# Down projections in products of 384 columns: three with the high weights in place of four of 288

## The chip, the cores and the metric

The kernel runs on one core of one Trainium2 chip. The metric is the device time of one execution in microseconds, the median of several; lower is better.

## The reference, cut to what matters

One inference step of a two-layer decoder trunk on 512 prompt tokens and 64 sample tokens (8 sequences of 8), so 576 columns of activations, with a model width of 1024. It has four feed-forward blocks of this form, which are the part that is changed:

```python
def swiglu(h, w_gu, w_d):              # D_FF = 2816
    gu = h @ w_gu
    g, u = gu[..., :D_FF], gu[..., D_FF:]
    return (jax.nn.silu(g) * u) @ w_d

x = x + 0.5 * mod[:, 2, None] * swiglu(hh, ffn_w_gu[l, 0], ffn_w_d[l, 0])
```

Besides them there are a recurrent mixer (RG-LRU), one shared K/V projection, a differential-attention mixer with a paged cache, and norms with a shift, scale and gate per sequence. Everything is float32.

## The kernel before, in words

Activations lie transposed: 128 features on the partitions, 576 tokens along the row, `KT` = 8 such tiles for the width of 1024. For accuracy each float32 factor is split into a high and a low float32r part, and a product is made as high x high + high x low + low x high: weights `w_hi`, `w_lo`, activations `hh_hi`, `hh_lo` (after a norm) or `h_hi`, `h_lo` (inside a block).

A list, `plan`, holds the stages in order. An FFN is cut into three chunks of its inner width (8, 8 and 6 tiles). For each chunk an `up` stage makes the tiles of `h`, and a `down` stage multiplies them with the chunk's rows of the down weights and adds the result, times the gate, to the residual `x`. The last chunk's down stage (`sums=True`) also collects the sums for the next norm. The projections `w_out` and `w_o` of the two mixers are `down` stages with sums as well.

A stage consists of units. One unit is one weight block of 8 (or 6) k tiles by 256 columns, in two buffers by parity `j`: SyncE loads `raw[j]`, ScalarE rounds it to `w_hi[j]` (L808), VectorE subtracts to `w_lo[j]` (L1226), TensorE multiplies. A down stage has four units; each has two halves `t` (128 output features each). For each half and each k `tile_products` (L471 to L486) issues six float32r matmuls of 288 columns: for n = 0, 1 the high weights with the high and with the low part (L481), then the low weights with the high part for n = 0, 1 (L484). The results of half `t` accumulate in PSUM banks `2t` and `2t+1` (288 columns each). The weight is loaded anew for every matmul. "Group" below means the six products of one k and one half.

VectorE's `residual` takes a finished half: columns 0 to 287 (L1331), 288 to 511 (L1333), and the 64 sample columns in two steps through `r_tmp`, because their gate differs by sequence (L1337, L1341). The last of them frees the banks (`s0_free` for half 0, `s1_free` for half 1); TensorE waits for `s0_free` before half 0 of the next unit and for `s1_free` before its half 1. VectorE's order in a down unit is: split of the next unit's weights, residual of half 0, residual of half 1.

In the first unit of a down stage TensorE waits per k for `h_lo`, which GpSimd makes (L1654) from what VectorE (`hf`, L1385) and ScalarE (`h_hi`, L918) produced at the end of the up stage. Banks 4 and 5 are used by the conditioning projections ("bursts", L458 and L467) that are strewn over certain units; banks 6 and 7 by the norm statistics and by attention.

Of the kernel before, what the change touches and what calls it, by code (L numbers as in the profile page):

```python
# [30 lines left out]
P = 128  # L31
D_MODEL = 1024
SEQ = 512
# [19 lines left out]
PB = SEQ - TH  # L53
NC_ = 1 + DEC_BATCH
N_PAGES = PAST_LEN // PAGE
PADS = CONV_W - 1
# [50 lines left out]
def trunk(nc, consts, xT, page_table, ada_w, w_gu, w_d8, w_d6, w_in, w_gate, w_out, w_kv, w_q, w_o, k_cache, v_cache,  # L107
          yT, conv_out, h_out, kT_out, v_prompt, v_sample):
    plan = []
    count = {"u": 0, "norm": 0, "stat": 1, "h": 0, "res": 0, "rope": 0}  # L110

# [9 lines left out]
    def down(**more):  # L121

        stage("down", 4, row=0, **more)
        count["res"] += 8
        if more["sums"]:
            count["stat"] += 1

    def ffn(layer, which):
# [36 lines left out]
    with ExitStack() as ctx:  # L165
# [53 lines left out]
        def laid(key, below, *tensors):  # L219
            with ExitStack() as part:  # L220
# [10 lines left out]
        laid("linear", 0, ("hh_hi", [P, KT, T], F32R), ("hh_lo", [P, KT, T], F32R),  # L231
             ("h_hi", [P, KT, T], F32R), ("h_lo", [P, KT, T], F32R),
             ("ada", [P, GROUP, KT, 256], F32))
# [18 lines left out]
        R = region  # L252
        hh_hi, hh_lo, h_hi, h_lo = R["hh_hi"], R["hh_lo"], R["h_hi"], R["h_lo"]
        ada, ada_pro = R["ada"], R["ada_pro"]
# [51 lines left out]
        for name in ("cst_in", "x_in", "pt_in", "cond_ready", "setup_done", "setup_exp", "setup_step", "raw_full0",  # L306
                     "raw_full1", "w_hi", "out0_full", "ada_full", "pro_full", "ada_done", "ada_rows", "ada_evac",
                     "cst_late", "gate_ready", "c_zero", "os_rows", "rg_gelu", "ada_turned", "sq_full", "sq_sum",
                     "sq_last", "half_full", "res_half", "sums_full", "rstd_ready", "ln_ready", "mod_ready", "norm_t",
                     "norm_hi", "norm_lo", "norm_sv", "norm_sx", "norm_shi", "norm_s", "hh_free", "y_ready", "out_y",  # L310
                     "h_hi", "gw_full0", "gw_full1", "rope_swap", "rope_t2",
                     "kh_full0", "kh_full1", "vh_full0", "vh_full1", "sc_full", "masked",
                     "coef_ready", "att_part", "s_small", "k_full0", "k_full1", *[f"v_full{i}" for i in range(N_PAGES)],
                     "qbd_zero", "qbd_ready", "smasked", "smax", "snmx", "srs", "so_sq", "so_ln", "so_sum",
                     "so_rs", "so_n", "ss_sq", "ss_sum", "ss_ln", "ss_rs", "ss_n", "ss_hi", "ss_lo", "v_used",
                     "state_out",
                     "rg_pad", *CREDITS):
            sem(name)
# [127 lines left out]
        def _(pe):  # L446
# [24 lines left out]
            def tile_products(j, half_tile, rhs_hi, rhs_lo, s, k_tiles, ready, first, done):  # L471
# [14 lines left out]
                mm.then_inc(sems[done], 1)  # L486

            def part(j, t, n, k, rhs_hi, rhs_lo, k_tiles):

# [106 lines left out]
            for s in plan:  # L596
# [47 lines left out]
                if s["kind"] == "down":  # L644
                    h_all = s["h"]
                    for m in range(s["units"]):
                        kt = s["k"]
                        if s["sums"] and m == s["units"] - 1:
                            unit_with_sums(u0 + m, m % 2, kt, s["stat"])
                        else:  # L650
                            unit(u0 + m, m % 2, h_hi, h_lo, kt, "h_lo", h_all - kt, by_half=("loaded" in s and m == 0))
# [488 lines left out]
        def _(dve):  # L1140
# [181 lines left out]
            def residual(u, k, t, res, half=None):  # L1322
# [6 lines left out]
                else:  # L1329
# [12 lines left out]
                   .then_inc(sems["s1_free" if t else "s0_free"], 1)  # L1342

            def rope(u, t, r, scale, out, swap, a, b):

# [18 lines left out]
            for at, s in enumerate(plan):  # L1364
# [24 lines left out]
                if s["kind"] == "down":  # L1389
# [11 lines left out]
                    for m in range(s["units"]):  # L1401
# [5 lines left out]
                        for t in range(2):  # L1407
                            k = 2 * m + t
                            residual(u, k, t, s["res"] + k, s["stat"] if s["sums"] and k == KT - 1 else None)
                            if s["sums"] and k < KT - 1:  # L1410
                                add_square(s["stat"], k)
# [376 lines left out]
```

## Time and profile before

| | |
|---|---|
| time, median of 3 runs | 2484.01 us (2480.96 to 2487.26) |
| the profiled execution | 2485.17 us |
| its span, first to last instruction | 2483.3 us |
| TensorE busy | 2342.4 us, 94% |
| TensorE weight loads busy | 2212.3 us, 89% |
| VectorE busy | 984.8 us, 40% |
| ScalarE busy | 766.0 us, 31% |
| GpSimd busy | 152.4 us, 6% |
| mean granted TensorE clock | 0.981 |

Busy time is the time in which at least one instruction of the engine was recorded as running. Successive matmuls overlap in their records, so the mean duration of one (some 295 ns) is longer than the time from one start to the next; what a matmul costs in a stream is read from its start to the next start. The chain of waits follows the work that ended last backwards in time, and its pieces, listed in order of time, show where each piece began. Times in windows and timelines are microseconds from the start of the span.

### The profile page before, as it was taken

What the parts mean: (1) busy time and instruction counts of PE and PEld (TensorE: products, weight loads), DVE (VectorE), ACT (ScalarE), POOL (GpSimd) and SP (SyncE); (2) the same over time, 40 slices, a digit from 0 to 9 for tenths busy, and PEclk for the clock granted to TensorE, in tenths of its full rate; (3) what the DMA queues carried; (4) which work ended last, traced back from release to release, by engine and by line L of the source; (5) the groups of instructions that cost most, each with busy time, mean ns of one, the idle gap of its engine ahead of it and who ended that gap; (6) DMA issues with size and microseconds to landing.
All of it is one profiled execution on the core that took longest, in us unless ns stands there. A gap on an engine that the chain in (4) does not pass through costs nothing.

```text
span 2483.3 us, 41990 instructions
## 1 busy us (share of the span) xinstructions
PE 2342.4 (94%) x18402; PEld 2212.3 (89%) x18402; DVE 984.8 (40%) x1617; ACT 766.0 (31%) x1021; POOL 152.4 (6%) x125
## 2 busy tenths in 40 slices
PE   5999999999899999998989999998788899999998
PEld 4999999998789999998989999998644499999998
DVE  5222232587542322236342322326456654232325
ACT  4221212367332122124432122124434433212122
POOL 0000100000001010000001000010000100001000
PEclk9999999999899999999999999999899999999999
DMA  8432343212332432433432334322599511222221
GB/s 331 150 130 108 126 153 144 82 58 80 130 136 86 153 136 86 153 136 110 167 124 104 151 138 153 136 73 94 182 378 418 223 69 68 86 85 86 86 77 64
DMA packets 64553, 338.38 MB, mean 136 GB/s; under 512 B 8050, under 2 KB 12274, under 8 KB 34930
## 3 DMA queue, kind: packets, MB, share of 16 engines
q1 hardware_dynamic: 61426, 330.97, 35.3%
q10 hardware_dynamic: 2944, 4.72, 0.5%
q8 instruction: 145, 2.38, 0.4%
q14 instruction: 38, 0.31, 0.0%
HBM read 328.44 MB, written 7.23 MB: 135 GB/s over the span
## 4 chain that ended last, share of the span: by engine, by line
PE 83%; DVE 9%; ACT 4%; issue 2%; DMA 1%; SPq 1%; POOL 0%; DVEq 0%; ACTq 0%; POOLq 0%
PE ps L481 48%; PE ps L484 24%; PE ps L458 2%; PE ps L493 1%; DVE w_lo L1226 1%; PE ps L495 1%; PE ps L494 1%; ACT w_hi L808 1%; PE ps L695 1%; DMA ada_pro<-in_ada_w 1%; DVE xc L1440 1%; DVE hf L1261 1%; DVE hh_lo L1269 1%; PE ps L684 1%; PE ps L727 0%
## 5 line engine op out<-in xcount | busy, mean ns | idle before, releaser
L481 PE MATMUL ps<-hh_hi,w_hi 128*128 128x288 f32 x3200 | 900.6, 296 | 18.1 <-DVE w_lo L1226 7.8
L481 PE MATMUL ps<-hh_lo,w_hi 128*128 128x288 f32 x3200 | 900.4, 296 | 0.0
L484 PE MATMUL ps<-hh_hi,w_lo 128*128 128x288 f32 x3200 | 681.4, 294 | 0.0
L481 PEld LDWEIGHTS ps<-hh_hi,w_hi 128*128 128x128 f32 x3200 | 603.5, 189 | 24.8 <-issue 9.9
L481 PEld LDWEIGHTS ps<-hh_lo,w_hi 128*128 128x128 f32 x3200 | 603.9, 189 | 0.1
L484 PEld LDWEIGHTS ps<-hh_hi,w_lo 128*128 128x128 f32 x3200 | 515.6, 189 | 0.0
L1226 DVE TENSOR_TENSOR w_lo<-raw,w_hi 128x2048 fp32r<-128x2048 f32 x164 | 375.9, 2292 | 315.6 <-ACT w_hi L808 304.3
L481 PE MATMUL ps<-h_hi,w_hi 128*128 128x288 f32 x1568 | 440.2, 295 | 11.4 <-POOL h_lo L1654 11.4
L481 PE MATMUL ps<-h_lo,w_hi 128*128 128x288 f32 x1568 | 440.6, 296 | 0.0
L808 ACT ACTIVATE w_hi<-raw 128x2048 fp32r<-128x2048 f32 x164 | 312.8, 1907 | 324.9 <-PE ps L484 313.8
L484 PE MATMUL ps<-h_hi,w_lo 128*128 128x288 f32 x1568 | 332.9, 293 | 0.0
L1385 DVE TENSOR_TENSOR hf<-sg,ps 128x576 f32<-128x576 f32 x88 | 66.3, 754 | 641.3 <-PE ps L484 640.1
L481 PEld LDWEIGHTS ps<-h_hi,w_hi 128*128 128x128 f32 x1568 | 295.0, 188 | 14.0 <-POOL h_lo L1654 11.9
L481 PEld LDWEIGHTS ps<-h_lo,w_hi 128*128 128x128 f32 x1568 | 295.1, 188 | 0.1
L1654 POOL TENSOR_TENSOR h_lo<-hf,h_hi 128x576 fp32r<-128x576 f32 x96 | 137.4, 1431 | 1981.7 <-ACT h_hi L918 1802.9
L484 PEld LDWEIGHTS ps<-h_hi,w_lo 128*128 128x128 f32 x1568 | 252.1, 188 | 0.0
L918 ACT ACTIVATE h_hi<-hf 128x576 fp32r<-128x576 f32 x88 | 60.4, 686 | 550.7 <-DVE hf L1385 550.7
L1331 DVE SCALAR_TENSOR_TENSOR x<-ps,mod_g,x 128x288 f32<-128x288 f32 x106 | 54.8, 517 | 272.7 <-PE ps L484 271.8
L914 ACT ACTIVATE sg<-ps 128x576 f32<-128x576 f32 x88 | 57.3, 652 | 274.9 <-PE ps L484 273.4
L493 PE MATMUL ps<-hh_hi,w_hi 128*128 128x288 f32 x256 | 85.7, 335 | 28.3 <-DVE hh_lo L1269 24.1
L493 PEld LDWEIGHTS ps<-hh_hi,w_hi 128*128 128x128 f32 x256 | 53.5, 209 | 34.0 <-issue 26.9
L833 ACT ACTIVATE sg<-x 128x576 f32<-128x576 f32 x49 | 33.5, 685 | 160.0 <-DVE x L1341 150.6
(207 smaller groups left out, 1775.0 us busy)
## 6 DMA issues: line engine op xcount, KB each, us to landing
raw<-in_w_gu SPq DMA_DIRECT2D x88, 1024.0 KB, 4.8
ada<-in_ada_w SPq DMA_DIRECT2D x76, 1024.0 KB, 10.8
raw<-in_w_d SPq DMA_DIRECT2D x32, 1024.0 KB, 4.8
kr<-in_k_cache SPq DMA_DIRECT2D x64, 512.0 KB, 6.9
vr<-in_v_cache SPq DMA_DIRECT2D x64, 512.0 KB, 6.9
raw<-in_w_d SPq DMA_DIRECT2D x16, 768.0 KB, 4.3
raw<-in_w_in SPq DMA_DIRECT2D x8, 1024.0 KB, 5.1
raw<-in_w_kv SPq DMA_DIRECT2D x8, 1024.0 KB, 4.8
```

What stands on the lines that cost most here:

```text
L458: mm = pe.matmul(ps[32 * t:32 * t + 32, 4 + g % 2, 0:256], act_c[:, k, :], tile[:, t, k, :], start=(k == 0), stop=(k == KT - 1))
L481: pe.matmul(ps[:, 2 * s + n, 0:TH], whi, r[:, k, TH * n:TH * n + TH], start=(k == 0 and r is rhs_hi), stop=False)
L484: mm = pe.matmul(ps[:, 2 * s + n, 0:TH], wlo, rhs_hi[:, k, TH * n:TH * n + TH], start=False, stop=(k == k_tiles - 1))
L493: pe.matmul(out, whi, rhs_hi[:, k, cols], start=(k == 0), stop=False)
L808: act.activation(w_hi[j][:, :, :].rearrange("p k n -> p (k n)"), raw[j][:, :], ACT.Copy)\
L833: act.activation(sg[k % 2][:, :], x[:, k, :], ACT.Square).then_inc(sems["sq_full"], 1)
L914: act.activation(halves(sg[j][:, :]), slot(0), ACT.Silu).then_inc(sems["s0_free"], 1)
L918: act.activation(h_hi[:, 2 * i + j, :], hf[j][:, :], ACT.Copy).then_inc(sems["h_hi"], 1)
L1226: dve.tensor_tensor(w_lo[j][:, :, :].rearrange("p k n -> p (k n)"), raw[j][:, :], w_hi[j][:, :, :].rearrange("p k n -> p (k n)").bitcast(F32),
L1331: dve.scalar_tensor_tensor(x[:, k, 0:TH], ps[:, 2 * t, 0:TH], mod_g[:, k, 0:1], x[:, k, 0:TH], ALU.mult, ALU.add)
L1385: dve.tensor_tensor(halves(hf[j][:, :]), halves(sg[j][:, :]), slot(1), ALU.mult)\
L1654: pool.tensor_tensor(lo[:, k, :], tile[:, :], hi[:, k, :].bitcast(F32), ALU.subtract)\
```

## The change

In the down stages without sums (the first two chunks of each FFN, so 8 stages of 4 units) a group is made by `wide_products`. `h_hi` and `h_lo` become the two halves of one tensor `h_both`, so that one operand can reach from one into the other. The high part and the low part together have 2 x 576 = 1152 columns, all to be multiplied with the same high weights; they are now cut into three products of 384: high columns 0 to 383 into bank `2t`; a middle product, called the seam below, of high columns 384 to 575 and low columns 0 to 191 into bank `6 + t`; low columns 192 to 575 into bank `2t + 1`. The low weights still make two products of 288 columns with the high part, accumulated into banks `2t` and `2t + 1` at the columns they belong to. From k = 1 on the two low-weight products come first in the group.

`wide_residual` has to put the parts together: columns 0 to 191 come from bank `2t` alone for the high part and from the seam's second piece for the low part, and so on. It has four multiply-adds of 384, 128, 192 and 320 columns, and for the 64 sample columns a copy, an add of two sums, a multiply and an add, with semaphores between those that touch the same data. All other stages keep `tile_products` and `residual`.

```diff
--- before.py
+++ after.py
@@ -52,6 +52,7 @@
 TH = T // 2
 PB = SEQ - TH
 NC_ = 1 + DEC_BATCH
+WIDE = 384
 N_PAGES = PAST_LEN // PAGE
 PADS = CONV_W - 1
 SEG = PADS + DEC_SEQ
@@ -107,7 +108,7 @@
 def trunk(nc, consts, xT, page_table, ada_w, w_gu, w_d8, w_d6, w_in, w_gate, w_out, w_kv, w_q, w_o, k_cache, v_cache,
           yT, conv_out, h_out, kT_out, v_prompt, v_sample):
     plan = []
-    count = {"u": 0, "norm": 0, "stat": 1, "h": 0, "res": 0, "rope": 0}
+    count = {"u": 0, "norm": 0, "stat": 1, "h": 0, "res": 0, "rope": 0, "wide": 0}
 
     def stage(kind, units=0, **more):
         plan.append({"kind": kind, "units": units, **count, **more})
@@ -121,9 +122,11 @@
     def down(**more):
 
         stage("down", 4, row=0, **more)
-        count["res"] += 8
         if more["sums"]:
+            count["res"] += 8
             count["stat"] += 1
+        else:
+            count["wide"] += 8
 
     def ffn(layer, which):
         tile0 = L1_TILE0 * layer
@@ -229,7 +232,7 @@
         w_lo.append(region["w_lo1"])
         hh = KT * T
         laid("linear", 0, ("hh_hi", [P, KT, T], F32R), ("hh_lo", [P, KT, T], F32R),
-             ("h_hi", [P, KT, T], F32R), ("h_lo", [P, KT, T], F32R),
+             ("h_both", [P, 2, KT, T], F32R),
              ("ada", [P, GROUP, KT, 256], F32))
         laid("ada_first", 2 * hh, ("ada_pro", [P, GROUP, KT, 256], F32))
 
@@ -250,7 +253,8 @@
              ("pp0", [P, 2, SEQ], F32), ("pp1", [P, 2, SEQ], F32))
         laid("weights", 4 * hh + N_HEADS * (T + 144 + S_TOK), ("probs", [P, PAST_LEN + S_TOK], F32))
         R = region
-        hh_hi, hh_lo, h_hi, h_lo = R["hh_hi"], R["hh_lo"], R["h_hi"], R["h_lo"]
+        hh_hi, hh_lo, h_both = R["hh_hi"], R["hh_lo"], R["h_both"]
+        h_hi, h_lo = h_both[:, 0, :, :], h_both[:, 1, :, :]
         ada, ada_pro = R["ada"], R["ada_pro"]
         xp, xc, th_r, th_i = R["xp"], [R["xc0"], R["xc1"]], R["th_r"], R["th_i"]
         tau, dec, dec2, hs, gv, gt, gy = R["tau"], R["a"], R["a2"], R["hs"], R["gv"], R["gt"], [R["gy0"], R["gy1"]]
@@ -313,7 +317,7 @@
                      "coef_ready", "att_part", "s_small", "k_full0", "k_full1", *[f"v_full{i}" for i in range(N_PAGES)],
                      "qbd_zero", "qbd_ready", "smasked", "smax", "snmx", "srs", "so_sq", "so_ln", "so_sum",
                      "so_rs", "so_n", "ss_sq", "ss_sum", "ss_ln", "ss_rs", "ss_n", "ss_hi", "ss_lo", "v_used",
-                     "state_out",
+                     "state_out", "wide_hi", "wide_t", "wide_s",
                      "rg_pad", *CREDITS):
             sem(name)
 
@@ -485,6 +489,40 @@
                                        start=False, stop=(k == k_tiles - 1))
                 mm.then_inc(sems[done], 1)
 
+            def wide_products(j, t, k_tiles, ready, first, done):
+
+                for k in range(k_tiles):
+                    if ready:
+                        pe.wait_ge(sems[ready], first + k + 1 + CREDITS[ready])
+                    whi, wlo = w_hi[j][:, k, P * t:P * t + P], w_lo[j][:, k, P * t:P * t + P]
+                    at = h_hi[:, k, WIDE:T]
+                    seam = bass.AP(at.tensor, at.offset, [list(at.ap[0]), [KT * T - WIDE, 2], [1, WIDE // 2]])
+                    out_a, out_c = ps[:, 2 * t, 0:WIDE], ps[:, 2 * t + 1, 0:WIDE]
+                    out_b = ps[:, 6 + t, 0:WIDE].rearrange("p (a b) -> p a b", a=2)
+                    begin, end = k == 0, k == k_tiles - 1
+                    if not begin:
+                        pe.matmul(ps[:, 2 * t, 0:TH], wlo, h_hi[:, k, 0:TH], start=False, stop=False)
+                        pe.matmul(ps[:, 2 * t + 1, WIDE - TH:WIDE], wlo, h_hi[:, k, TH:T], start=False, stop=False)
+                    pe.matmul(out_a, whi, h_hi[:, k, 0:WIDE], start=begin, stop=end)
+                    pe.matmul(out_b, whi, seam, start=begin, stop=end)
+                    mm = pe.matmul(out_c, whi, h_lo[:, k, T - WIDE:T], start=begin, stop=end)
+                    if begin:
+                        pe.matmul(ps[:, 2 * t, 0:TH], wlo, h_hi[:, k, 0:TH], start=False, stop=False)
+                        pe.matmul(ps[:, 2 * t + 1, WIDE - TH:WIDE], wlo, h_hi[:, k, TH:T], start=False, stop=False)
+                mm.then_inc(sems[done], 1)
+
+            def wide_unit(u, j, k_tiles, first):
+
+                pe.wait_ge(sems["w_lo"], u + 1 + CREDITS["w_lo"])
+                pe.wait_ge(sems["s0_free"], u + CREDITS["s0_free"])
+                wide_products(j, 0, k_tiles, "h_lo" if j == 0 else None, first, "out0_full")
+                if u in BURSTS:
+                    ada_burst(BURSTS[u])
+                pe.wait_ge(sems["s1_free"], u + CREDITS["s1_free"])
+                wide_products(j, 1, k_tiles, None, 0, "w_done")
+                if u in BURSTS:
+                    ada_turn(BURSTS[u])
+
             def part(j, t, n, k, rhs_hi, rhs_lo, k_tiles):
 
                 cols = slice(TH * n, TH * n + TH)
@@ -647,6 +685,8 @@
                         kt = s["k"]
                         if s["sums"] and m == s["units"] - 1:
                             unit_with_sums(u0 + m, m % 2, kt, s["stat"])
+                        elif not s["sums"]:
+                            wide_unit(u0 + m, m % 2, kt, h_all - kt)
                         else:
                             unit(u0 + m, m % 2, h_hi, h_lo, kt, "h_lo", h_all - kt, by_half=("loaded" in s and m == 0))
                     if s["last"]:
@@ -1340,6 +1380,31 @@
                 dve.wait_ge(sems["res_tmp"], res + 1 + CREDITS["res_tmp"])
                 dve.tensor_tensor(x[:, k, SEQ:T], r_tmp, x[:, k, SEQ:T], ALU.add)\
                    .then_inc(sems["s1_free" if t else "s0_free"], 1)
+
+            def wide_residual(u, k, t, r):
+
+                dve.wait_ge(sems["w_done" if t else "out0_full"], count("w_done" if t else "out0_full", u + 1))
+                a, b, d = ps[:, 2 * t, 0:WIDE], ps[:, 6 + t, 0:WIDE], ps[:, 2 * t + 1, 0:WIDE]
+                gain, half = mod_g[:, k, 0:1], WIDE // 2
+                dve.scalar_tensor_tensor(x[:, k, 0:WIDE], a, gain, x[:, k, 0:WIDE], ALU.mult, ALU.add)\
+                   .then_inc(sems["wide_hi"], 1)
+                dve.wait_ge(sems["wide_s"], r)
+                dve.tensor_copy(r_tmp, b[:, SEQ - WIDE:half]).then_inc(sems["wide_t"], 1)
+                dve.scalar_tensor_tensor(x[:, k, WIDE:SEQ], b[:, 0:SEQ - WIDE], gain, x[:, k, WIDE:SEQ],
+                                         ALU.mult, ALU.add).then_inc(sems["wide_hi"], 1)
+                dve.wait_ge(sems["wide_t"], 3 * r + 1)
+                dve.tensor_tensor(r_tmp, r_tmp, d[:, SEQ - half:WIDE], ALU.add).then_inc(sems["wide_t"], 1)
+                dve.wait_ge(sems["wide_hi"], 2 * r + 1)
+                dve.scalar_tensor_tensor(x[:, k, 0:half], b[:, half:WIDE], gain, x[:, k, 0:half], ALU.mult, ALU.add)
+                dve.wait_ge(sems["wide_t"], 3 * r + 2)
+                dve.tensor_tensor(by_seq(r_tmp), by_seq(r_tmp),
+                                  mod_g[:, k, 1:NC_].unsqueeze(2).to_broadcast([P, DEC_BATCH, DEC_SEQ]),
+                                  ALU.mult).then_inc(sems["wide_t"], 1)
+                dve.wait_ge(sems["wide_hi"], 2 * r + 2)
+                dve.scalar_tensor_tensor(x[:, k, half:SEQ], d[:, 0:SEQ - half], gain, x[:, k, half:SEQ],
+                                         ALU.mult, ALU.add).then_inc(sems["s1_free" if t else "s0_free"], 1)
+                dve.wait_ge(sems["wide_t"], 3 * r + 3)
+                dve.tensor_tensor(x[:, k, SEQ:T], r_tmp, x[:, k, SEQ:T], ALU.add).then_inc(sems["wide_s"], 1)
 
             def rope(u, t, r, scale, out, swap, a, b):
 
@@ -1406,7 +1471,10 @@
                             modulation(plan[at + 1])
                         for t in range(2):
                             k = 2 * m + t
-                            residual(u, k, t, s["res"] + k, s["stat"] if s["sums"] and k == KT - 1 else None)
+                            if s["sums"]:
+                                residual(u, k, t, s["res"] + k, s["stat"] if k == KT - 1 else None)
+                            else:
+                                wide_residual(u, k, t, s["wide"] + k)
                             if s["sums"] and k < KT - 1:
                                 add_square(s["stat"], k)
                         if u in BURSTS:
```

## Rows read from the trace of the kernel before

**Rows 1.** The page: busy times and the chain's shares.
```profile
PE 2342.4 (94%) x18402; PEld 2212.3 (89%) x18402; DVE 984.8 (40%) x1617; ACT 766.0 (31%) x1021; POOL 152.4 (6%) x125
...
PE 83%; DVE 9%; ACT 4%; issue 2%; DMA 1%; SPq 1%; POOL 0%; DVEq 0%; ACTq 0%; POOLq 0%
PE ps L481 48%; PE ps L484 24%; PE ps L458 2%; PE ps L493 1%; DVE w_lo L1226 1%; PE ps L495 1%; PE ps L494 1%; ACT w_hi L808 1%; PE ps L695 1%; DMA ada_pro<-in_ada_w 1%; DVE xc L1440 1%; DVE hf L1261 1%; DVE hh_lo L1269 1%; PE ps L684 1%; PE ps L727 0%
```

**Rows 2.** The page: groups; count, busy us, mean ns.
```profile
L481 PE MATMUL ps<-h_hi,w_hi 128*128 128x288 f32 x1568 | 440.2, 295 | 11.4 <-POOL h_lo L1654 11.4
L484 PE MATMUL ps<-h_hi,w_lo 128*128 128x288 f32 x1568 | 332.9, 293 | 0.0
```

**Rows 3.** Windows: busy us (count) per engine, granted clock, DMA share.
```profile
39.00:45.00 6.00, 4.81 (x20) 4.84 (x21) 5.77 (x14) 3.80 (x8) 0.00 (x0) 0.50 1.01 427
317.60:330.40 12.80, 12.80 (x99) 12.80 (x98) 4.28 (x6) 2.50 (x2) 1.44 (x1) 1.00 0.78 307
330.40:342.90 12.50, 12.50 (x99) 12.50 (x98) 4.76 (x9) 1.92 (x1) 0.00 (x0) 1.00 0.23 85
```

**Rows 4.** Chain, down units of chunk 1: start us, us, what.
```profile
320.14 0.54 PE ps L481 x4
320.94 0.54 PE ps L481 x4
...
333.66 0.53 PE ps L481 x4
334.18 0.26 PE ps L484 x2
334.44 0.53 PE ps L481 x4
```

**Rows 5.** Timeline of TensorE, one group, odd unit: start us, us.
```profile
330.38 0.29 PE L481 MATMUL ps<-h_hi,w_hi 128*128 128x288 f32 x1
330.50 0.29 PE L481 MATMUL ps<-h_lo,w_hi 128*128 128x288 f32 x1
330.63 0.29 PE L481 MATMUL ps<-h_hi,w_hi 128*128 128x288 f32 x1
```

**Rows 6.** Timeline of TensorE at the lower clock.
```profile
41.53 0.44 PE L495 MATMUL ps<-hh_hi,w_lo 128*128 128x288 f32 x1
...
41.77 0.44 PE L493 MATMUL ps<-hh_hi,w_hi 128*128 128x288 f32 x1
```

**Rows 7.** Timelines and groups: float32 products of L610, weight loads of L714.
```profile
519.46 2.18 PE L610 MATMUL ps<-xc,nt 128*128 128x300 f32 x8
...
L610 PE MATMUL ps<-xc,nt 128*128 128x300 f32 x8 | 2.2, 415 | 0.0
...
1810.44 1.64 PEld L714 LDWEIGHTS ps<-small,probs 128*128 128x128 f32 x14
...
L714 PEld LDWEIGHTS ps<-small,probs 128*128 128x128 f32 x128 | 14.9, 192 | 0.6
```

**Rows 8.** Timeline of VectorE, down units of chunk 1.
```profile
324.18 0.52 DVE L1331 SCALAR_TENSOR_TENSOR x<-ps,mod_g,x 128x288 f32<-128x288 f32 x1 [0.79 <-PE ps L484]
...
325.22 0.22 DVE L1341 TENSOR_TENSOR x<-small,x 128x64 f32<-128x64 f32 x1
330.58 0.52 DVE L1331 SCALAR_TENSOR_TENSOR x<-ps,mod_g,x 128x288 f32<-128x288 f32 x1 [5.13 <-PE ps L484]
...
332.59 2.29 DVE L1226 TENSOR_TENSOR w_lo<-raw,w_hi 128x2048 fp32r<-128x2048 f32 x1 [0.74 <-ACT w_hi L808]
```

**Rows 9.** Groups by form, down stage: count, busy us, mean ns.
```profile
L1331 DVE SCALAR_TENSOR_TENSOR x<-ps,mod_g,x 128x288 f32<-128x288 f32 x7 | 3.6, 517 | 22.0 <-PE ps L484 22.0
L1333 DVE SCALAR_TENSOR_TENSOR x<-ps,mod_g,x 128x224 f32<-128x224 f32 x7 | 3.1, 442 | 0.0
```

**Rows 10.** Timelines of GpSimd and ScalarE, same stage.
```profile
319.33 1.44 POOL L1654 TENSOR_TENSOR h_lo<-hf,h_hi 128x576 fp32r<-128x576 f32 x1 [11.65 <-ACT h_hi L918]
...
330.63 1.92 ACT L808 ACTIVATE w_hi<-raw 128x2048 fp32r<-128x2048 f32 x1 [9.57 <-PE ps L484]
```

## Prediction

> **What bounds the kernel now.** I read the page first: busy shares and chain. TensorE is busy 94% of 2483.3 us and is 83% of the chain that ended last, and two lines, L481 and L484, are 72% of it; VectorE is busy 40% [rows 1]. The costliest groups then say what kind of work that is: float32r products of 288 columns, each with weights of its own, and the down projections have 1568 each of high by high, high by low and low by high at L481 and L484 [rows 2]. The windows of two down units of chunk 1 show TensorE busy in all of 12.80 us and all of 12.50 us, at a granted clock of 1.00, with VectorE busy in 4.28 and 4.76 [rows 3]. So in the stretch that is changed nothing is late but TensorE itself: what the edit is worth is what it does to the time of one group of products.
>
> That time is read from the chain of waits in the same stretch. One group (a weight tile k and a half t: four products with high weights, two with low) takes 320.94 - 320.14 = 0.80 us in an even unit and 334.44 - 333.66 = 0.78 in an odd one [rows 4], all groups of a unit alike. The mean is 790 ns for six products, 131.7 each; the starts of single products are 0.12 to 0.13 us apart [rows 5]. Their durations (0.29 us) are no price: they overlap, and the step from start to start is what is paid.
>
> **What is in the 131.7 ns.** The chip grants one of two levels. At the lower one (0.50, so 1.2 GHz) the same products start every 0.24 us [rows 3, 6], which is 288 columns / 1.2 GHz with nothing on top. At the upper level 288 / 2.4 GHz = 120 ns, so 131.7 has 11.7 ns on top (13.3 in even units, 10.0 in odd ones). The plain float32 products of L610 stand in the trace as two records per call, each of 300 columns at half the rate (300 / 1.2 = 250 ns), and start (2.18 - 0.42) / 7 = 251 ns apart: 1 ns on top [rows 7]. The weight load alone is a floor of (1.64 - 0.19) / 13 = 112 ns, seen where the product has 64 columns [rows 7]; 131.7 is above that, and a 384-column product (160 ns at 2.4 GHz) further still. So the 11.7 ns belong to float32r at the upper clock; whether they come once per product or grow with its columns, no row says, since every float32r product here has 288 columns.
>
> **The change part by part.**
> Where it applies: four FFNs, two chunks each, four units, two halves, eight k: 4 x 2 x 4 x 2 x 8 = 512 groups. The third chunk (six tiles, with sums), w_out and w_o keep the old form.
> Products: a group had 6 x 288 = 1728 columns and gets 3 x 384 + 2 x 288 = 1728. The streamed time, 720 ns, stays; one product in six goes, with its weight load. If the 11.7 ns are paid once per product, the group goes to 3 x (160 + 11.7) + 2 x 131.7 = 778.5, which is 11.7 less: 512 x 11.7 = 6.0 us (5.1 by the odd units' 10.0, 6.8 by the even units' 13.3). If they grow with columns (131.7 / 288 = 0.457 ns a column) the group stays at 790: nothing gained. If they vanish at 384 columns, because something that needs about 130 ns per product lies beside a longer stream, a product of 384 costs as float32 shows, 160 + 1 to 2, so 162: 3 x 162 + 263.4 = 749.4, and 512 x 40.6 = 20.8 us go. I take the first: the ends are 0 and 20.8, the step depends on which weight buffer is loaded (0.80 against 0.78 for the same columns), which points to something that happens once per product and load rather than at every column.
> The Trainium skill, "TensorE: Matmul & The Clock Gate", section "Back-to-back issue gap", gives a step of N/2.4 + 2.5 ns at full clock; by it a group would go from 735 to 732.5 ns and the change would be worth 512 x 2.5 = 1.3 us. The trace's 131.7 for 288 columns [rows 4, 5] is not the rule's 122.5, so I do not sum by it, but it speaks against a gain.
> Seam: the middle product reads 192 columns of the high part and 192 of the low part, which stand far apart in SBUF. No product in the trace reads two float32r pieces. Bound: nothing, or a restart as a product of its own has, 11.7 ns, 512 x 11.7 = 6.0 us. I take nothing; below nothing has no reason. Output banks: seam sums go to banks 6 and 7, idle in these stages; the statistics' products that use them come only with sums. Nothing.
> Order: low-weight products come first from k = 1 on. Same loads, same waits; nothing.
> VectorE: the residual of a half has now four operations, from 324.18 to 325.44 [rows 8]. Afterwards eight: multiply-adds of 384, 128, 192 and 320 columns, and a copy, an add, a multiply and an add of 64. From 517 ns for 288 columns and 442 for 224 [rows 9] the slope is 1.2 ns a column, so 630 + 330 + 405 + 555 = 1.92 us, and four times 0.21 to 0.23 = 0.87, in all 2.8 instead of 1.3 us, some waits on its own operations among it: 1.5 us more, 64 times, 96 us of VectorE. It is hidden: the banks of the first half, free at 325.44, are wanted by the next unit at 330.3, 4.8 us later; and what is queued behind the second half's residual (from 330.58, 1.3 us long as the first) is the split of the low weights, which starts at 332.59 because it waits for ScalarE's w_hi, begun at 330.63, and is wanted only at about 342.9 [rows 3, 8, 10]. It would slip to about 333.5, seven microseconds early still. If the cover were gone it would show as a TensorE gap at each half.
> First unit of a stage: it waits for h_lo per k; the last one is finished at 319.33 + 1.44 = 320.8 and is wanted at the eighth group, 317.7 + 7 x 0.8 = 323.3 [rows 4, 10]. Unchanged at a group of 0.78.
> The two names h_hi and h_lo as halves of one tensor lie where they lay. 1024 fewer TensorE instructions to fetch: nothing visible, TensorE doesn't wait for its queue in these windows.
> Sum: -6.0 us on the profiled execution's 2485.17 us (span 2483.3 and 1.9 around it), 2479.2. That execution lies 1.2 above the median of the three runs, 2484.01; off that the time is 2478.0.
>
> **The rivals.**
> (A) Forecast, one overhead per product: 2478, own range 2474 to 2482. For it: cold products have no overhead, buffer-dependent steps. Against it: float32 products at the same clock have next to none. Chance 0.43.
> (B) The overhead grows with columns: the stream of float32r at the upper clock is simply slower than 2.4 GHz. For it: at half the rate per column (cold, or float32) it is gone, as a limit on the rate would make it. Against: 0.78 against 0.80 at the same columns. The gain is nothing, at most 1 ns a group: 2484. Chance 0.24. The rule quoted above would look the same in the result.
> (C) Something of about 130 ns per product, hidden by 160 ns of stream: 2484 - 20.8 = 2463. For it: cold and float32 products, both longer than 130, show nothing on top, just as it would have it. Against: the load alone is good for 112 ns. Values between it and A are likelier than the full price. Chance 0.22.
> (D) Slower. The seam: the jump between high and low part stops the stream as the start of a product does, or for longer, in each of 512 groups. It outweighs A from 11.7 ns on and B from nothing. With B's rate and one restart it is +6 us, 2490; with two such (one more for the product behind it) +12, 2496. For it: no such operand is in the trace. Against: the stream passes from one product to the next with only 11.7 ns. Chance 0.11.
> That the change doesn't do what it says, that is that the same columns are spread over as many products, is excluded by the diff: five matmuls stand in the loop.
>
> **How the numbers follow.** The time is A's: 2478. The range for 8 in 10 takes A and B whole, the part of C that lies between it and A, and the near half of D: 2464 to 2489; scatter of the runs of some 2 us is in it. What can be told from no change is about 0.3%, 7.5 us. Faster by more: C nearly whole (0.20), and of A the part in which each product's overhead is above its mean or the median of the runs falls low (0.17): 0.37. Slower by more: of D the dearer half and scatter, 0.07. Within: 0.56.
>
> **What the profile after would show.** In the chain, a group of a chunk-0 or chunk-1 down unit: 0.77 and 0.79 us by A, 0.78 and 0.80 by B, 0.74 to 0.76 by C, over 0.80 by D. Steps after a 384-column product: 0.172, 0.175, 0.162 us; after the seam product alone, 0.18 and more by D. TensorE busy throughout such a window; if VectorE's sums were late there would be idle time with "DVE x" as releaser. VectorE busy 1.0 to 1.1 ms in all instead of 984.8 us. Groups on hh_hi, untouched, stay at 0.78 and 0.80; if these moved too, my reading of the overhead is wrong. The prediction falls if the group moves by more than 20 ns, or if a gap opens at the halves.

## The result, and the profile after

The changed kernel takes 2478.76 us (median of 11 runs, 2474.18 to 2483.26) against 2484.34 us before (11 runs, 2480.96 to 2487.26): ratio 0.9977 with a 95% interval of 0.9967 to 0.9986, so 5.6 us less, 3.5 to 8.2. A second comparison (run e12 below) gives 2478.17 against 2483.65, ratio 0.9978 (0.9969 to 0.9987). Forecast were 2478.0 us and 6.0 us less. The total is right; the reason given for it is mostly not, as the experiments show.

The page of the kernel after, its counterpart to [rows 1] and [rows 2] (L485 and L488 are L481 and L484 of before; L504 to L508 are the new group):

```profile
PE 2337.3 (94%) x17890; PEld 2206.2 (89%) x17890; DVE 1043.2 (42%) x1873; ACT 765.9 (31%) x1021; POOL 152.5 (6%) x125
...
PE 83%; DVE 9%; ACT 4%; issue 2%; DMA 1%; SPq 0%; POOL 0%; DVEq 0%; ACTq 0%; POOLq 0%
PE ps L485 37%; PE ps L488 18%; PE ps L506 4%; PE ps L507 4%; PE ps L508 4%; PE ps L462 3%; PE ps L505 2%; PE ps L504 2%; DVE w_lo L1266 1%; ACT w_hi L848 1%; PE ps L531 1%; PE ps L735 1%; PE ps L533 1%; PE ps L532 1%; DVE hf L1301 1%
...
L506 PE MATMUL ps<-h_both,w_hi 128*128 128x384 f32 x512 | 173.3, 338 | 0.0
L507 PE MATMUL ps<-h_both,w_hi 128*128 128x384 f32 x512 | 171.6, 335 | 0.0
...
L505 PE MATMUL ps<-h_both,w_lo 128*128 128x288 f32 x448 | 131.6, 294 | 0.0
```

The reader sees 512 products fewer (18402 to 17890, one for each of the 512 groups), 58 us more of VectorE, and the same shares in the chain: nothing has taken TensorE's place. The windows of two down units of chunk 1, the counterpart of [rows 3], have it busy throughout at a granted clock of 1.00:

```profile
317.60:330.20 12.60, 12.60 (x83) 12.60 (x82) 5.36 (x13) 3.13 (x3) 1.43 (x1) 1.00 0.70 282
330.40:342.90 12.50, 12.50 (x81) 12.50 (x81) 6.49 (x18) 1.83 (x2) 0.00 (x0) 1.00 0.24 85
```

What a group costs stands in TensorE's timeline (start, duration). First an even unit, from the first low-weight product of one group to that of the next:

```profile
319.97 0.29 PE L504 MATMUL ps<-h_both,w_lo 128*128 128x288 f32 x1
320.09 0.29 PE L505 MATMUL ps<-h_both,w_lo 128*128 128x288 f32 x1
320.23 0.34 PE L506 MATMUL ps<-h_both,w_hi 128*128 128x384 f32 x1
320.40 0.33 PE L507 MATMUL ps<-h_both,w_hi 128*128 128x384 f32 x1
320.57 0.34 PE L508 MATMUL ps<-h_both,w_hi 128*128 128x384 f32 x1
320.75 0.29 PE L504 MATMUL ps<-h_both,w_lo 128*128 128x288 f32 x1
...
332.46 0.29 PE L504 MATMUL ps<-h_both,w_lo 128*128 128x288 f32 x1
...
333.25 0.29 PE L504 MATMUL ps<-h_both,w_lo 128*128 128x288 f32 x1
```

The even unit takes 0.78 us a group (779 ns over a whole half), the odd one, the last two rows, 0.79 (787 ns). Before they took 0.80 and 0.78 [rows 4]. (In six of the 32 odd halves of these stages the kernel before took 790, behind a burst.) So the change takes 21 ns off a group in even units and adds 7 in odd ones: 7 ns net, not 11.7. The steps of the 384-column products are 0.17 to 0.18 us.

From the first product of each changed stage to the first of the next, summed over the eight stages: 425.92 us before, 422.07 after, 3.85 us less (0.41 to 0.59 a stage), and in the second profile of the change the same 3.85. The rest of the 6.3 us between the two spans lies in stages that the edit doesn't touch. The q stage with attention, for example, took 271.21 us before, 269.45 after, and anything from 268.06 to 272.61 in the profiles of the twelve runs below, which leave it alone. That is scatter between executions, and 3.85 us lies inside the interval of both comparisons.

### The profile page after: what moved, and what is told of

It reads as the page before. It is cut to its first block, busy times and chain, and to the rows that moved or that the text cites. A ratio compares the mean times of both kernels' runs of the same rounds, so it can differ in the third digit from the quotient of the medians.

```text
span 2477.0 us, 41222 instructions
## 1 busy us (share of the span) xinstructions
PE 2337.3 (94%) x17890; PEld 2206.2 (89%) x17890; DVE 1043.2 (42%) x1873; ACT 765.9 (31%) x1021; POOL 152.5 (6%) x125
## 4 chain that ended last, share of the span: by engine, by line
PE 83%; DVE 9%; ACT 4%; issue 2%; DMA 1%; SPq 0%; POOL 0%; DVEq 0%; ACTq 0%; POOLq 0%
PE ps L485 37%; PE ps L488 18%; PE ps L506 4%; PE ps L507 4%; PE ps L508 4%; PE ps L462 3%; PE ps L505 2%; PE ps L504 2%; DVE w_lo L1266 1%; ACT w_hi L848 1%; PE ps L531 1%; PE ps L735 1%; PE ps L533 1%; PE ps L532 1%; DVE hf L1301 1%
## 5 line engine op out<-in xcount | busy, mean ns | idle before, releaser
L485 PE MATMUL ps<-hh_hi,w_hi 128*128 128x288 f32 x3200 | 900.1, 296 | 17.5 <-DVE w_lo L1266 7.6
L485 PE MATMUL ps<-hh_lo,w_hi 128*128 128x288 f32 x3200 | 899.5, 296 | 0.0
L488 PE MATMUL ps<-hh_hi,w_lo 128*128 128x288 f32 x3200 | 680.9, 293 | 0.0
L485 PEld LDWEIGHTS ps<-hh_hi,w_hi 128*128 128x128 f32 x3200 | 602.9, 188 | 24.2 <-issue 9.3
L485 PEld LDWEIGHTS ps<-hh_lo,w_hi 128*128 128x128 f32 x3200 | 603.1, 188 | 0.1
L488 PEld LDWEIGHTS ps<-hh_hi,w_lo 128*128 128x128 f32 x3200 | 514.8, 188 | 0.0
L1722 POOL TENSOR_TENSOR h_both<-hf,h_both 128x576 fp32r<-128x576 f32 x96 | 137.5, 1433 | 1977.0 <-ACT h_both L958 1798.5
L958 ACT ACTIVATE h_both<-hf 128x576 fp32r<-128x576 f32 x88 | 60.4, 686 | 551.0 <-DVE hf L1450 551.0
L485 PE MATMUL ps<-h_both,w_hi 128*128 128x288 f32 x1088 | 190.4, 297 | 11.4 <-POOL h_both L1722 11.4
L506 PE MATMUL ps<-h_both,w_hi 128*128 128x384 f32 x512 | 173.3, 338 | 0.0
L507 PE MATMUL ps<-h_both,w_hi 128*128 128x384 f32 x512 | 171.6, 335 | 0.0
L508 PE MATMUL ps<-h_both,w_hi 128*128 128x384 f32 x512 | 171.6, 335 | 0.0
L485 PEld LDWEIGHTS ps<-h_both,w_hi 128*128 128x128 f32 x1088 | 160.2, 190 | 12.0 <-POOL h_both L1722 11.9
L505 PE MATMUL ps<-h_both,w_lo 128*128 128x288 f32 x448 | 131.6, 294 | 0.0
L504 PE MATMUL ps<-h_both,w_lo 128*128 128x288 f32 x448 | 131.2, 293 | 0.0
L1389 DVE SCALAR_TENSOR_TENSOR x<-ps,mod_g,x 128x384 f32<-128x384 f32 x64 | 39.5, 618 | 200.9 <-PE ps L508 200.9
L488 PE MATMUL ps<-h_both,w_lo 128*128 128x288 f32 x544 | 116.0, 294 | 0.0
```

The source lines that it names most:

```text
L485: pe.matmul(ps[:, 2 * s + n, 0:TH], whi, r[:, k, TH * n:TH * n + TH], start=(k == 0 and r is rhs_hi), stop=False)
L488: mm = pe.matmul(ps[:, 2 * s + n, 0:TH], wlo, rhs_hi[:, k, TH * n:TH * n + TH], start=False, stop=(k == k_tiles - 1))
L504: pe.matmul(ps[:, 2 * t, 0:TH], wlo, h_hi[:, k, 0:TH], start=False, stop=False)
L505: pe.matmul(ps[:, 2 * t + 1, WIDE - TH:WIDE], wlo, h_hi[:, k, TH:T], start=False, stop=False)
L506: pe.matmul(out_a, whi, h_hi[:, k, 0:WIDE], start=begin, stop=end)
L507: pe.matmul(out_b, whi, seam, start=begin, stop=end)
```

## The experiments

Twelve kernels ran. Those with a single execution (e1 to e4, e7 to e10) are read by steps and stage times in the trace, which repeat from kernel to kernel to some 0.01 us a stage where nothing was edited and no norm or attention is in the stage.

**e1, a scan of widths.** In each of the eight wide stages the three high-weight products read W contiguous columns.

```diff
+WIDTHS = (None, 384, 512, 448, 320, 256, 192, 128)
...
+    if width:
+        w = max(width, WIDE) if begin else width
+        pe.matmul(ps[:, 2 * t, 0:w], whi, flat[:, T * k:T * k + w], start=begin, stop=False)
+        pe.matmul(ps[:, 6 + t, 0:w], whi, flat[:, T * k:T * k + w], start=begin, stop=end)
+        pe.matmul(ps[:, 2 * t + 1, 0:w], whi, flat[:, T * k:T * k + w], start=begin, stop=False)
```

> The three high-weight products of a group read one contiguous piece of W columns, another W in each of the eight wide stages: seam form as in the change, then 384 contiguous, 512, 448, 320, 256, 192, 128 (k = 0 keeps 384 at least). The sums that the down stages form are therefore not those of the reference. What is read is the step from the start of such a product to the next start. Theory 1, a fixed cost per product of some 13 ns: 512 gives 226 ns, 448 gives 200, 384 gives 173, 320 gives 146, 256 gives 120, and 192 and 128 rest on the 112 ns floor of the weight load. Theory 2, the overhead grows with columns (0.453 ns a column, as 174 / 384 and 131.7 / 288 nearly have it): 512 gives 232, 448 gives 203, 320 gives 145, 256 gives 116 to 118. Theory 3, part and part, a line through 131.7 at 288 and 174 at 384 (slope 0.44): 512 gives 230, 256 gives 117. The seam stage against the contiguous 384: same step by my prediction, 11.7 ns more for the seam product by the rival that it restarts the stream.

One group in the stage of 512 columns, then one in that of 256, from TensorE's timeline:

```profile
815.47 0.39 PE L507 MATMUL ps<-h_both,w_hi 128*128 128x512 f32 x1
815.69 0.39 PE L508 MATMUL ps<-h_both,w_hi 128*128 128x512 f32 x1
815.92 0.40 PE L509 MATMUL ps<-h_both,w_hi 128*128 128x512 f32 x1
816.16 0.29 PE L510 MATMUL ps<-h_both,w_lo 128*128 128x288 f32 x1
...
1556.39 0.28 PE L507 MATMUL ps<-h_both,w_hi 128*128 128x256 f32 x1
1556.51 0.28 PE L508 MATMUL ps<-h_both,w_hi 128*128 128x256 f32 x1
1556.63 0.28 PE L509 MATMUL ps<-h_both,w_hi 128*128 128x256 f32 x1
1556.74 0.29 PE L510 MATMUL ps<-h_both,w_lo 128*128 128x288 f32 x1
```

512 columns: (816.16 - 815.47) / 3 = 0.23 us a product; 256: (1556.74 - 1556.39) / 3 = 0.117. The same quotient as a mean over the groups of the stage from its halves' second weight tile on (with e10's beside it):

```
columns                 256     320     384     448     512
e1, mean step, ns     117.6   145.9   173.6   203.7   232.0
e10, mean step, ns    117.7   145.2   174.8   204.4   232.0
2.3 + 0.450 x columns 117.5   146.3   175.1   203.9   232.7
```

Lines fitted to the rows of 256, 320, 448 and 512 columns are 2.9 + 0.448 x columns for e1 and 2.1 + 0.450 x columns for e10; the line of the table is used below, and its 2.3 ns stand for 2 to 3, since single groups scatter by up to 3 ns a product about these means. It gives 131.9 at 288 columns, where the kernel before has 131.7, and 175.1 at 384, where the groups of 779 and 787 ns leave 172 to 174. So about 2.3 ns are paid once per product (with its weight load) and 0.450 - 0.417 = 0.033 ns more than 2.4 GHz would take for every column. My prediction's fixed 11.7 ns is refuted (it needs 226 at 512). Theory 2 holds within 1 ns; of theory 3 the form is right, but its slope of 0.44 puts too much on the product (230 at 512). At 192 and 128 columns the three steps average 104.3 and 93.8 ns, far above 89 and 60, and a group takes 600 ns at either width, 120 for each of its five products: there the weight loads, which start 0.11 us apart where they are closest, bound the group, as [rows 7] had it.

The first two stages of this kernel are the seam and 384 contiguous columns: 54.35 and 54.22 us, where the change has 54.35 and 54.27. The jump from the high to the low part costs at most 0.05 us in 64 groups, under 1 ns each, and the groups of both forms take the same 779 and 787 ns. Rival (D) is gone.

**e9, is it the weight load beside the stream?** In one up stage of each FFN the weights of k = 1 to 6 are cut.

```diff
+CUTS = (P, 32, 64, 96, 16)
...
+    m = P if k in (0, k_tiles - 1) else CUTS[cut]
+    whi, wlo = whi[:, 0:m], wlo[:, 0:m]
```

> The change, and in the middle chunk of each FFN's up stage (old form, 288 columns) the weights of k = 1 to 6 are cut from 128 columns to 32, 64, 96 and 16 (by FFN), so that the load beside each product is shorter; the results of these chunks are therefore not those of the reference. Theory 1, the overhead over 120 ns comes from the weight load beside the stream (its reads or its switch): the step falls with the cut, to 122 to 124 ns at 32 columns. Theory 2, float32r at the upper clock streams at less than 2.4 columns a nanosecond whatever lies beside it: the step stays at 130 to 133 ns.

```profile
L491 PEld LDWEIGHTS ps<-hh_hi,w_lo 128*32 128x32 f32 x158 | 17.1, 108 | 3.6
...
240.17 0.30 PE L488 MATMUL ps<-hh_hi,w_hi 128*32 128x288 f32 x1
240.30 0.30 PE L488 MATMUL ps<-hh_lo,w_hi 128*32 128x288 f32 x1
...
240.97 0.29 PE L488 MATMUL ps<-hh_hi,w_hi 128*32 128x288 f32 x1
```

A load of 32 columns is 108 ns long instead of 188, and the group still takes 240.97 - 240.17 = 0.80 us. Over all their products the steps are 131.7, 131.3, 130.9 and 132.2 ns at 16, 32, 64 and 96 weight columns; with 128 columns the change has 131.6, 131.9, 131.7 and 132.0 in the same four stages. The length of the load beside it is not what holds the stream back.

**e10, the same scan with other addresses.** e1 with the padding of e5.

> The width scan of e1 (so again sums that are not the reference's) with the address residues of e5: both weight buffers and the activations at 128 modulo 256. Theory, overhead mostly per column: the same line, 0.445 ns a column and some 3.4 ns a product, within 2 ns at each width. Rival, the slope of e1 is an effect of its addresses: at 512 columns the step differs by 5 ns or more from e1's 231.

The table above: within 0.7 ns at the four widths of the line and 1.2 at 384. (The 0.445 and 3.4 of this expectation are an earlier reading of e1.) The line is not an effect of where the buffers lie.

**e4, positions.** The odd weight buffers and all activations lie 128 bytes further on.

```diff
+        laid("odd_unit", None, ("odd_pad", [P, PAD], F32), ("w_hi1", ...
...
-                    sb("below_" + key, [P, 2 * UNIT + below], F32, part)
+                    sb("below_" + key, [P, 2 * UNIT + PAD + below], F32, part)
```

> The change, with the odd weight buffers and all activations 128 bytes further in SBUF; the even weight buffers stay. Theory 1 (cost per product, position of no matter): groups as before, 0.80 even and 0.78 odd on hh, 0.783 in the wide ones. Rival, the 10 ns between even and odd units come from the addresses of the buffers relative to the activations: the pattern of even and odd changes, and with it the time by up to 0.6%.

The time is 2495.85 us in one run, 17 us above the change's median. The chain of an up stage that the change leaves alone, even unit first, then an odd one:

```profile
218.49 0.54 PE ps L486 x4
219.03 0.27 PE ps L489 x2
219.30 0.54 PE ps L486 x4
...
224.09 0.52 PE ps L486 x4
224.88 0.52 PE ps L486 x4
225.68 0.52 PE ps L486 x4
```

0.81 us in even and 0.79 in odd units (807 and 790 ns over whole halves) where the change has 800 and 780; wide groups average 787 to 790 in even units and 787 in odd ones, where the change has 779 and 787. The same products on the same data cost another 7 to 10 ns a group for 128 bytes of shift, in every FFN of the trace, so the position of the buffers does matter. My theory said it would not.

**e5 and e6, all buffers at one residue.** Before the change the even weight buffers lie at 64 and the odd ones and the activations at 128 modulo 256 bytes, if one counts the allocations. Padding puts all at 128; e5 does it to the change, e6 to the kernel before.

```diff
+        sb("pad0", [P, 16])
         raw = [sb(f"raw{j}", [P, UNIT]) for j in range(2)]
...
         h_sb = sb("h_sb", [P, KT, NC_])
+        sb("pad1", [P, 48])
```

> The change with 64 bytes of padding ahead of the weight buffers (and 192 behind, so that all else stays where it was modulo 256 bytes): the even weight buffers now lie, modulo 256, where the odd ones and the activations lie. Theory (addresses set the overhead): old-form groups of even units fall from 0.80 to 0.78 like those of odd ones; wide groups of even units rise from 779 to 787 ns like the odd ones; in all some 55 even units x 16 x 20 ns less and 16 x 16 x 8 ns more, so about 15 us less than the change, 2463 us. Rival (a cost per product that has nothing to do with addresses; the even and odd difference comes from something else that alternates): 2478 as the change.

> The kernel before with the same padding, so six products of 288 columns everywhere. Theory: all groups 0.78, the time some 4 us below that of e5, since the wide form has 787 there: with aligned buffers the change costs time instead of saving it, 2459 to 2461 us. Rival, one overhead saved per group whatever the addresses: 6 us above e5.

Measured: e5 2479.62 us (ratio to before 0.9990, 0.9981 to 1.0000), e6 2483.70 (1.0007, 0.9998 to 1.0017). Both times and group times miss the expectation; the rivals come nearer in time (2478, and 6 us between the two, measured 4.1), but not in the groups, since even and odd units now agree. The chains of the same up stage, first e5, then e6:

```profile
210.87 0.52 PE ps L487 x4
...
211.67 0.52 PE ps L487 x4
...
212.45 0.52 PE ps L487 x4
```
```profile
213.51 0.52 PE ps L483 x4
...
214.31 0.52 PE ps L483 x4
...
215.09 0.52 PE ps L483 x4
```

Two groups take 1.58 us in both: 790 ns in even and odd units of this stage, not 780. So the padding evened out the units and gained nothing in the mean. It does give the cleanest pair for the change itself: in the five of the eight wide stages in which e6 has 790 throughout, e5 takes 0.20 to 0.21 us less (54.60 against 54.80, for one), 0.20 us in 64 groups or 3.1 ns a group (787 against 790), near the 2.3 ns that the line gives for one product fewer. In eight stages that would be 1.6 us, less than half of the 3.85. Of the others one is 0.05 longer, because three halves of e6's stage run at 780, and the last two are 1.3 shorter, because of what the last fence of this part shows. And the trace of e6 holds a third fact, read from its last FFN:

```profile
2360.29 0.54 PE ps L483 x4
2361.10 0.54 PE ps L483 x4
2361.90 0.54 PE ps L483 x4
```

Here the same code with the same addresses runs at 0.81 (807 ns), while its K/V stage ran at 780. The first up stage of the second FFN, which e5 and e6 have alike in code and addresses, runs at 807 in e5 and at 780 in e6. So a group doesn't have its time from the addresses alone; it also stays in what it fell into before: in these two kernels the value changes only behind a break in the stream of groups. The medians of e5 and e6 hold such differences too, so the clean reading is that of the five stages.

**e7 and e8, two more sets of residues.** Only the paddings differ.

> The change with other address residues modulo 256: even weight buffers at 160, odd at 0, activations at 128 (in the change 64, 128, 128). Theory: the group times differ between even and odd units and are none of them tied to the count of products; a distance between weights and activations of 0 was the best so far (780), so both should be above 780 in the old form. Rival: 780 and 800 as before.

> The change with residues modulo 256 of 64 (even weights), 192 (odd weights) and 64 (activations). If the distance between weights and activations alone decides, the even units now have 780 (distance 0). If the place of the activations matters too (at 0 with weights at 0 it was 790, not 780), the even units have another value than 780. Rival: 780 and 800 as before.

e7: 2489.98 us in one run, old groups 793 (even) and 787 and 793 in turn (odd), wide ones 793 and 787. e8: 2483.46 us in one run, old groups mostly 790 (even) and 787 and 793 in turn (odd), with one stage that changes between 800 and 780; wide ones mostly 787 and 807, with halves at 780 and 800. A distance of 0 gives 790 here and in e5, and gave 780 in the odd units of before. No set tried has 780 throughout, and distance alone does not decide.

**e2, other orders of the six products.** Each triple is weight part, activation part and column half, with 0 for high; the first order is the usual one.

```diff
+ORDERS = (((0, 0, 0), (0, 1, 0), (0, 0, 1), (0, 1, 1), (1, 0, 0), (1, 0, 1)),
+          ((1, 0, 0), (1, 0, 1), (0, 0, 0), (0, 1, 0), (0, 0, 1), (0, 1, 1)),
+          ((0, 0, 0), (0, 0, 1), (0, 1, 0), (0, 1, 1), (1, 0, 0), (1, 0, 1)),
+          ((0, 0, 0), (0, 1, 0), (1, 0, 0), (0, 0, 1), (0, 1, 1), (1, 0, 1)),
+          ((0, 0, 0), (0, 1, 1), (1, 0, 0), (0, 1, 0), (0, 0, 1), (1, 0, 1)))
```

> The change, and in the middle chunk of each FFN's up stage (untouched six products of 288 columns) another order of the six: low weights first; high0 high1 low0 low1; by column half; and one in which every product changes both bank and part. Theory 1, the overhead is paid once per product whatever surrounds it: groups stay at 0.78 in odd and 0.80 in even units in each of the four. Rival, the steps come from how one product's reads follow another's: the group differs between the orders, by 10 ns or more, and the order of the change's wide group explains part of its 783 ns.

Groups of even and odd units: low weights first 800 and mostly 807, high0 high1 low0 low1 793 and 795 to 805, by column half 793 and 800, all changing 800 and 807, against 800 and 780 in the usual order. So the order matters, by up to 27 ns in odd units, and none was better in the mean. Low weights first, which is also how a wide group begins, is worse by 27 in odd units: the change's odd units lose while its even ones gain, but that the order is the cause of it was not tried in the wide form itself.

**e3, VectorE's cover.** 6 more small memsets before each half's residual in every further stage.

```diff
+                for _ in range(6 * (r // 8)):
+                    dve.wait_ge(sems["fill"], fills[0])
+                    dve.memset(filler[:, :], 0.0).then_inc(sems["fill"], 1)
...
```

> The change, with 0, 6, 12, ... 42 chained small memsets on VectorE before the residual of each half, by stage: the cover of the longer residual is used up step by step. By the prediction (1.5 us more per half are hidden, some 3 us are left in a half) the first stages with up to some 3 us of filler take 50.1 or 54.3 us as without it, and only then gaps of TensorE open with DVE x as releaser. Rival: VectorE's residual is already late in the change and costs part of the gain, so that the very first filler lengthens its stage.

```profile
981.10 4.56 DVE L1392 MEMSET filler<- 128x128 f32 x18
985.57 0.50 DVE L1396 SCALAR_TENSOR_TENSOR x<-ps,mod_g,x 128x384 f32<-128x384 f32 x1
...
987.42 0.21 DVE L1414 TENSOR_TENSOR x<-small,x 128x64 f32<-128x64 f32 x1
...
L507 PE MATMUL ps<-h_both,w_hi 128*128 128x384 f32 x62 | 21.7, 351 | 2.8 <-DVE x L1411 2.8
```

A memset takes 4.56 / 18 = 0.25 us. With 0, 6 and 12 of them (up to 3.0 us) the stages take 54.35, 54.27 and 54.35 us, the same as without; with 18 (4.5 us) the fourth takes 60.41 instead of 54.35, and L507 waits for VectorE's L1411, the releaser that I named. That wait is 2.8 us of the 6.1; a part of the rest is the granted clock, 0.66 from 1005 to 1010 us, behind the longest wait. The longer residual was hidden, with at least 3.0 us of room a half.

**e11, the wide form in even units alone,** since only they gain.

```diff
-                        elif not s["sums"]:
+                        elif not s["sums"] and m % 2 == 0:
                             wide_unit(...)
...
```

(Left out: the waits on `r_tmp`, which the two kinds of residual now share.)

> The change in the even units of the eight stages alone; the odd units keep six products and the old residual. By the group times of the change (even 800 to 779, odd 780 to 787 ns): 256 x 21 = 5.4 us less than before, 1.8 us less than the change in these stages, 50.8 - 54.x us a stage accordingly; in the median 2477 if the change has 2479. Rival, what a group costs depends on the one before, so that odd units after even wide ones no longer have 780: no gain over the change.

```profile
333.09 0.52 PE ps L485 x4
333.62 0.26 PE ps L488 x2
333.88 0.52 PE ps L485 x4
...
334.67 0.52 PE ps L485 x4
```

An odd unit in old form between wide ones now takes 0.79 us a group (12.65 us a unit), where the same code between old ones took 0.78. The eight stages take 2.85 us less than before instead of 5.4. Its rival holds: what a group costs depends on what ran before. 2479.14 us, ratio 0.9982 (0.9973 to 0.9991), no better than the change.

**e12, the change once more.**

> The change once more, beside e11 on the same chip. Its stages: 3.85 us less than before in the sum of the eight, as in the first profile, since these stages are exact to 0.1 us; the rest of the span moves by some 3 us either way between executions, and the median should be 4 to 6 us below before.

2478.17 us, the eight stages 3.85 us shorter, as expected. No kernel of the study that does the same work beats the change beyond its interval (e1 and e10, at 2457.08 and 2464.56 us, stream fewer columns).

## Why the prediction was right, and where not

*The bound.* Right. TensorE stays busy throughout the changed stages, a step of it is what counts, and group times x 512 give the stages' gain: 7 x 512 = 3.6 us of the 3.85.

*The count.* Right: 512 groups, 1728 columns each as before, 512 products fewer on the page.

*The price of a product.* This step failed, and the total hid it. "The 11.7 ns are paid once per product" was chosen against "grows with columns", and e1 shows 2.3 ns per product and the rest by columns. As a description of the stream rival (B), at 0.24, was the better one, and by its "at most 1 ns a group" it too is off. My argument for (A) was that even and odd units differ at equal columns. The observation was sound, the conclusion was not: that difference belongs to positions and history (e4, e5, e6, e11), with which an old group settles anywhere from 780 to 807 ns. The numbers then met by luck: 512 x 11.7 = 6.0 us forecast; 2.3 ns x 512 = 1.2 us for the product, and another 2.7 us because the new group settles at 779 and 787 where the old had 800 and 780. That split is shown; why the new group settles there (its order, its three banks, or where its operands lie) is not. Measured are 3.85 us in the stages; the median fell by 5.6 (3.5 to 8.2), and the rest is not shown to be the change's.

*The rule of N/2.4 + 2.5 ns.* The Trainium skill, "TensorE: Matmul & The Clock Gate", section "Back-to-back issue gap", states it, as the gap of isolated products. Its constant agrees with the 2.3 ns measured in e1 and e10; its 1/2.4 ns a column does not hold for their float32r products, which take 0.450. The rule spoke against the change's gain and was nearer to the mechanism than my sum.

*The vanishing overhead.* (C) fell: 384 columns cost 172 to 174 ns in the change, not 162.

*The seam.* Costed at nothing, measured under 1 ns. Right.

*VectorE.* 2.8 us a half were estimated, 2.2 measured (323.28 to 325.47), 58 us more in all instead of 96, all hidden, with the room that the prediction gave. Right in kind, but the addition was 1.5 us a half by my sum and is 0.9: in their records the eight operations overlap by some 0.1 us each, and I added full durations.

*The check that I named.* "Groups on hh_hi, untouched, stay at 0.78 and 0.80." Most do, but of 200 such halves ten have another value in the profile after than before. The two units behind the second changed stage take 793 and 790 ns instead of 800 and 780, in both profiles of the change and not in e11, which ends that stage in the old form. And the first unit of the second FFN, 790 before, has 807 in the first profile of the change and 780 in that of e12, the same kernel (chains of the first, then of e12):

```profile
714.03 0.54 PE ps L485 x4
714.84 0.54 PE ps L485 x4
...
714.12 0.53 PE ps L485 x4
714.90 0.53 PE ps L485 x4
```

By my own words, "if these moved too, my reading of the overhead is wrong", this was a sign against (A). The even and odd values of the wide groups, forecast 0.79 and 0.77 and found 0.78 and 0.79, were another. The sentence "all groups of a unit alike" holds in the units of [rows 4], not in the whole trace.

Open is what holds float32r below 2.4 columns a nanosecond at the upper clock, and what makes a group settle at one of its values. The length of the weight load is excluded by e9; by e3, more work on VectorE leaves the groups alone (779 and 787 ns as long as TensorE doesn't wait).

## What to carry to other kernels

When all products of a trace have one width, their overhead can't be split into a part per product and a part per column, and the two give opposite advice; one kernel with a scan of widths settles it. Here joining products at constant columns is worth 2 to 3 ns each, so it pays only where it costs nothing elsewhere. And a gain of 1% in a stream of float32r products is no larger than what a shift of buffers or another order does to it (780 to 807 ns a group): compare versions in more than one placement before believing in the reason.

## What was not expected of the hardware

A float32r stream at the granted clock of 1.00 takes 0.450 ns a column from 256 to 512 columns, 8% more than the 0.417 of 2.4 GHz; plain float32 products, at half the rate, come within 1 ns of theirs (251 against 250 ns for 300 columns) [rows 7]. At a granted clock of 0.50 it keeps 240 ns for 288 columns to the nanosecond [rows 6]. A group of identical products has several steady times (780, 790, 793, 800 and 807 ns were seen), which change with the position of its buffers, the order within it and what ran before; with 128 bytes of shift the whole took 17 us longer in one run.
